# Adaptive modulation moved out of the sparse attention: 192 fp32 matmuls replaced by 192 scaled adds on VectorE and 48 one-column matmuls in the first feed-forward

## The chip, the cores and the metric

One Trainium2 chip, one core of it. The time is the device time of one execution in microseconds (us); the number that counts is the median of the runs.

## The reference, cut to what matters

Two transformer blocks follow each other on a sequence of 1024 tokens of width 1024. The first block has three attention branches and a feed-forward; the second is modulated by a condition vector.

```python
# first block: sliding-window, sparse ("dsa") and memory attention, gated and projected
x = x + einsum("bsd,de->bse", merged, w_out)
h = rmsnorm(x, g_mlp)
x = x + einsum("bsf,fd->bsd", square(relu(h @ w_mlp_in)), w_mlp_out)   # 1024 -> 4096 -> 1024
x = rmsnorm(x, g_final)
# second block
c_act = silu(c)                                   # 1024 numbers
mod = c_act @ w_ada + b_ada                       # (1024) x (1024, 6144) -> 6144 numbers
sh1, sc1, gt1, sh2, sc2, gt2 = split(mod, 6)
x = x + gt1 * mixer(modulate(rmsnorm(x, g_mix), sh1, sc1))
x = x + gt2 * ff(modulate(rmsnorm(x, g_ffn), sh2, sc2))
```

`mod` is a product of one row with a matrix of 24 MB. It depends on nothing that the first block computes, and the second block needs it only when that begins.

## The kernel before

Everything is fp32. The large products run on TensorE (PE) in three passes over split operands: `group` calls `product` (lines 1578 to 1580: high by high, low by high, high by low), 512 columns a pass, and the splits are made by ScalarE (ACT, `split_hi`, line 598: the high part) and VectorE (DVE, `split_lo`, line 972: the rest), from four raw weight tiles of 256 KB that SyncE (SP) loads. A tile is loaded again once its low part is made. The kernel is written by hand: each engine has one program, waits are on semaphores, and the order on each engine and each DMA queue is the order in the code.

**The sparse attention** works in 32 units: eight blocks of 128 queries by four heads. Block b has (b+1) x 128 keys. In turn u the PE program issues `dsa_scores(u+1)` (line 1782), then `dsa_transposes(u-1)` (line 1792), then `dsa_out(u-2)` (line 1804: probabilities by values). DVE masks the scores of unit u (`dsa_masked`: lines 1213 or 1209, the maximum in 1217, its negative in 1218) and normalizes unit u-1 (`dsa_normalized`, lines 1225 and 1226). ACT takes the exponentials of unit u (738) and copies the transposed probabilities of u-1 out of PSUM (748). At the end of a block, ACT copies the output (`oT_hi`, 762) and DVE makes its low part (`oT_lo`, 1237); this DVE step stands between the masking of a unit and the normalization of the one before.

**The modulation before.** In turns 8 to 31, between the scores and the transposes, PE also issues eight fp32 matmuls (line 1817). Each has a 128x24 window of a wide, mostly zero tile with silu(c) in one column as its weights and 256 columns of `w_ada` as its moving operand, so that 24 turns fill a 24x256 tile in `bank3`. The weights come as 24 DMAs of 1 MB on SP's queue (line 346), double buffered against the matmuls; eight loads of attention results (`o_in`, line 349) stand between them, and the first loads of the gates (`stage`, line 363) behind them. After the last unit DVE adds the bias (1245), PE transposes the rows (1826), DVE copies them to `modc` (1247), and only then (`ada_ok`) does PE begin the gated projections; POOL writes the rows to DRAM (`mod_d`, 507), from which two gates are later read back, broadcast to 128 partitions.

**The first feed-forward** (`ff` with k = 0) runs in eight chunks. A chunk has eight groups of 24 passes into `bank0` to `bank3`, one for each hidden tile (two halves of the tokens by four tiles of 128), and 16 groups of 12 passes, two for each of eight token tiles t. ACT takes relu, square and the high part of a hidden tile (791, 793, 797); DVE makes its low part (`hidden`, line 1302), then the low parts of the next chunk's first matrix (972), then adds the 16 results to `xs` (1327). PE may begin a group when DVE has freed the bank (`group_free`, raised in 1329) four groups before. Chunks 1 to 6 are a loop on DVE, chunks 1 to 7 one on PE.

## Time and profile before

| | |
|---|---|
| median of 3 runs | 3069.17 us (3067.54 to 3070.76) |
| the profiled execution | 3071.32 us |
| its span, first to last instruction | 3069.5 us |
| mean granted TensorE clock | 0.957 |
| sparse attention, up to its last `oT_lo` | about 671 to 871.7 us |
| gated projections | 872.9 to about 978 us |
| first feed-forward | about 1100 to 1790 us |

The profile is of one execution. Busy times are shares of its span; PE's ends are modelled, so the distance from start to start is the better measure of a pass. A chain of waits is followed back from the last instruction. The granted clock is a share of 2.4 GHz.

### The profile page before, as it was taken

How to read it: one execution, taken by the hardware profiler on the slowest of the kernel's cores; microseconds unless marked ns; L12 is line 12 of the kernel's file. 1: busy time of each engine (PE TensorE's matmuls, PEld its weight loads, DVE VectorE, ACT ScalarE, POOL GpSimd, SP SyncE). 2: the span in 40 equal slices, each digit the busy share in tenths (PEclk: the TensorE clock that was granted, in tenths of full speed). 3: DMA queues.
4: the chain of work that ended last, by engine and by line, in shares of the span. 5: the costliest groups of instructions: out<-in, count | busy, mean ns of one | idle time of the engine just before them, and what ended most of it. 6: DMA issues, size and time to landing. Idle time of an engine off the chain costs nothing.

```text
span 3069.5 us, 36159 instructions
## 1 busy us (share of the span) xinstructions
PE 2824.8 (92%) x13038; PEld 2257.7 (74%) x13038; DVE 1432.1 (47%) x2841; ACT 927.0 (30%) x1894; POOL 262.3 (9%) x430
## 2 busy tenths in 40 slices
PE   5996799989997989999999989998697999999997
PEld 4764678864575878888888866877686788888886
DVE  5286489973434242333223352335743443443445
ACT  5165232222211242222223343323414222332221
POOL 0222321220023000000000000003100000000000
PEclk9998889989998999999999998999798999999999
DMA  4012122326435110111011112220221111111111
GB/s 158 19 35 67 35 67 94 103 98 228 146 104 187 52 55 28 55 55 55 27 55 55 41 59 72 77 79 29 83 103 35 55 45 38 55 55 38 44 41 62
DMA packets 119646, 213.99 MB, mean 70 GB/s; under 512 B 10852, under 2 KB 39100, under 8 KB 119284
## 3 DMA queue, kind: packets, MB, share of 16 engines
q1 hardware_dynamic: 107188, 185.30, 18.3%
q10 hardware_dynamic: 8064, 14.68, 1.3%
q0 software_dynamic: 4288, 12.64, 1.3%
q8 instruction: 61, 1.00, 0.1%
q14 instruction: 45, 0.37, 0.0%
HBM read 178.94 MB, written 33.64 MB: 69 GB/s over the span
## 4 chain that ended last, share of the span: by engine, by line
PE 78%; DVE 9%; ACT 5%; DMA 3%; issue 2%; POOL 1%; SPq 0%; DVEq 0%; ACTq 0%; POOLq 0%
PE bank L1578 22%; PE bank L1579 22%; PE bank L1580 22%; PE bank L1817 3%; ACT w_hi L598 1%; PE bank L1804 1%; PE bank L1782 1%; DVE w_lo L972 1%; DVE stage L1256 1%; DVE probs L1077 1%; DMA w_raw<-in_w_mlp_in 1%; DMA w_raw<-in_w_ff 1%; PE bank L1792 1%; DVE mx L1063 1%; ACT bank L830 1%
## 5 line engine op out<-in xcount | busy, mean ns | idle before, releaser
L1578 PE MATMUL bank<-h_hi,w_hi 128*128 128x512 f32 (+1 forms) x1312 | 514.0, 392 | 18.3 <-DVE h_lo L1370 7.9
L1579 PE MATMUL bank<-h_lo,w_hi 128*128 128x512 f32 (+1 forms) x1312 | 511.7, 390 | 0.0
L1580 PE MATMUL bank<-h_hi,w_lo 128*128 128x512 f32 (+1 forms) x1312 | 511.2, 390 | 0.0
L598 ACT ACTIVATE w_hi<-w_raw 128x512 fp32r<-128x512 f32 (+3 forms) x440 | 254.9, 616 | 763.4 <-PE bank L1580 551.7
L1578 PE MATMUL bank<-w_hi,hid_hi 128*128 128x512 f32 x1024 | 400.9, 391 | 10.6 <-DVEq L1329 10.2
L1580 PE MATMUL bank<-w_hi,hid_lo 128*128 128x512 f32 x1024 | 399.4, 390 | 0.0
L1579 PE MATMUL bank<-w_lo,hid_hi 128*128 128x512 f32 x1024 | 399.4, 390 | 0.0
L972 DVE TENSOR_TENSOR w_lo<-w_raw,w_hi 128x512 fp32r<-128x512 f32 (+3 forms) x384 | 246.2, 680 | 211.6 <-ACT w_hi L598 205.8
L1302 DVE TENSOR_TENSOR hid_lo<-bank,hid_hi 128x512 fp32r<-128x512 f32 x128 | 88.6, 692 | 512.9 <-ACT hid_hi L797 512.9
L1578 PEld LDWEIGHTS bank<-h_hi,w_hi 128*128 128x128 f32 x1312 | 249.2, 190 | 73.5 <-DVE h_lo L1370 8.7
L1579 PEld LDWEIGHTS bank<-h_lo,w_hi 128*128 128x128 f32 x1312 | 249.2, 190 | 51.0 <-issue 0.7
L1580 PEld LDWEIGHTS bank<-h_hi,w_lo 128*128 128x128 f32 x1312 | 249.1, 190 | 51.0
L1327 DVE TENSOR_TENSOR xs<-xs,bank 128x512 f32<-128x512 f32 x256 | 175.9, 687 | 182.1 <-PE bank L1580 170.9
L1578 PEld LDWEIGHTS bank<-w_hi,hid_hi 128*128 128x128 f32 x1024 | 192.7, 188 | 56.3 <-DVEq L1329 16.9
L1580 PEld LDWEIGHTS bank<-w_hi,hid_lo 128*128 128x128 f32 x1024 | 192.7, 188 | 40.2
L1579 PEld LDWEIGHTS bank<-w_lo,hid_hi 128*128 128x128 f32 x1024 | 192.6, 188 | 39.6
L791 ACT ACTIVATE bank<-bank 128x512 f32<-128x512 f32 x128 | 74.5, 582 | 373.7 <-PE bank L1580 373.7
L1173 DVE TENSOR_SCALAR_CACHE_REDUCE cmpj<-isc,cand 128x384 bf16<-128x384 f32 (+1 forms) x186 | 175.8, 945 | 5.5
L1579 PE MATMUL bank<-hT_lo,w_hi 128*128 128x512 f32 x384 | 149.5, 389 | 0.0
L1580 PE MATMUL bank<-hT_hi,w_lo 128*128 128x512 f32 x384 | 149.5, 389 | 0.0
L1578 PE MATMUL bank<-hT_hi,w_hi 128*128 128x512 f32 x384 | 149.5, 389 | 0.0
L1325 DVE TENSOR_TENSOR bank<-bank,rowv 128x512 f32<-128x512 f32 x128 | 89.5, 699 | 106.6 <-PE bank L1580 94.5
(381 smaller groups left out, 3916.5 us busy)
## 6 DMA issues: line engine op xcount, KB each, us to landing
w_raw<-in_w_ff SPq DMA_DIRECT2D x128, 256.0 KB, 3.1
w_raw<-in_w_in SPq DMA_DIRECT2D x104, 256.0 KB, 2.9
ada<-in_w_ada SPq DMA_DIRECT2D x24, 1024.0 KB, 5.2
w_raw<-in_w_mlp_in SPq DMA_DIRECT2D x64, 256.0 KB, 3.1
w_raw<-in_w_mlp_out SPq DMA_DIRECT2D x64, 256.0 KB, 3.1
gates_scratch<-gstage ACTq DMA_DIRECT2D x48, 256.0 KB, 2.0
stage<-gates_scratch SPq DMA_DIRECT2D x16, 768.0 KB, 5.1
w_raw<-in_w_out SPq DMA_DIRECT2D x32, 256.0 KB, 3.7
```

The costliest lines, as they stand in the source:

```text
L598: A_(W[par][0][:, p, 0:n], raw[:, p % NRAW, 0:n], ACT.Copy).then_inc(w_hi, 1)
L791: A_(x, x, ACT.Relu).then_inc(f_r, 1)
L830: A_(x, x, ACT.Identity, scale=amod[:, a0 + k:a0 + k + 1], bias=modc[:, b0 + k:b0 + k + 1])\
L972: tt(W[par][1][:, p, 0:n], raw[:, p % NRAW, 0:n], W[par][0][:, p, 0:n].bitcast(f32), ALU.subtract).then_inc(w_lo, 1)
L1173: tsc(cmpj[:, 0:(b + 1) * P], isc[b][:, :], cand[:, b - 2:b - 1].bitcast(f32), None, ALU.is_ge, ALU.add, accum_out=cnt[:, b - 2:b - 1]).th ...
L1302: tt(hid[h][1][:, f, :], bank[n % 4][:, :], hid[h][0][:, f, :].bitcast(f32), ALU.subtract)\
L1325: tt(b, b, rowv[:, 512 * m:512 * m + 512], ALU.mult).then_inc(gt_x, 1)
L1327: tt(x, x, bank[(2 * t + m) % 4][:, :], ALU.add).then_inc(x_add, 1)
L1578: mm(out, lh, rh, start=(i == 0), stop=False)
L1579: mm(out, lh, rl, start=False, stop=False)
L1580: last = mm(out, ll, rh, start=False, stop=(i == n - 1))
L1817: l = mm(bank[3][0:NPC, 0:256], cwide[:, k, NPC - 1 - n:2 * NPC - 1 - n], adab[n % 2][:, k, :], start=(n == 0 and k == 0), stop=(n == NPC ...
```

## The change

- The 24 x 8 matmuls, the wide tile, the bias add in rows, the two transposes and the copy at the end of the attention are gone, and so are the 24 DMAs of 1 MB on SP's queue. The eight loads of attention results follow each other there, and the second gate load waits for the selection (`sel_done`) instead of the last of the matmuls.
- POOL now issues 96 DMAs of 256 KB (two row tiles of 128 by 256 columns each) into two small buffers in the place of `rowv`, behind its gate adds and the wait for the end of the attention. From the third on, each waits until DVE has used both row tiles of the load two before.
- In chunks 1 to 6 of the first feed-forward DVE computes four column tiles of 256 in each. A column tile is eight row tiles, each scaled by its number of silu(c) and added into `adac` (128x256). Four row tiles stand behind each of hidden tiles 0 to 5, eight behind tile 6.
- PE sums over the partitions: for each column tile, two matmuls with 128x128 of `adac` as weights and one column of ones, into two columns of `bank4`. They stand behind groups 2, 4 and 6 of the chunk and behind the two groups of token tile 0.
- After the feed-forward DVE adds the bias (now loaded with the other vectors and transposed) to `bank4` in one step. POOL loads the gain `g_final` after the last modulation load, and writes two gates to DRAM from columns, 4 bytes a piece.
- PE's loop is over chunks 1 to 6, and chunk 7 is written out behind it.

```diff
             for b in range(2):
                 sp.wait_ge(at_od[b], 16 * (NSWA + 8))
             sp.wait_ge(group_done, GP)
...
-            for n in range(24):
-                if n >= 2:
-                    sp.wait_ge(ada_mm, n - 1)
-                elif n == 1:
-                    sp.wait_ge(sel_done, 6)
-                sp.dma_start(adab[n % 2][:, :, :], ada[:, :, n * 256:(n + 1) * 256]).then_inc(ada_in[n % 2], 16)
-                if n >= 3 and attended:
-                    h, o, d, k0, k1 = attended.pop(0)
-                    sp.dma_start(o[:, k0:k1, :].bitcast(f32), d[k0 * P:k1 * P, h * HALF:(h + 1) * HALF]
-                                 .rearrange("(k p) q -> p k q", p=P)).then_inc(o_in, 16)
+            for h, o, d, k0, k1 in attended:
+                sp.dma_start(o[:, k0:k1, :].bitcast(f32), d[k0 * P:k1 * P, h * HALF:(h + 1) * HALF]
+                             .rearrange("(k p) q -> p k q", p=P)).then_inc(o_in, 16)
...
                 else:
-                    sp.wait_ge(ada_mm, 24)
+                    sp.wait_ge(sel_done, 6)
...
             pool.wait_ge(d_pv, 32)
+            ada = a["w_ada_2"][0].rearrange("(k p) n -> p k n", p=P)
+            for q in range(96):
+                n, k = q // 4, 2 * (q % 4)
+                if q >= 2:
+                    pool.wait_ge(ada_s, 2 * q - 2)
+                pool.dma_start(adab[q % 2][:, :, :], ada[:, k:k + 2, n * 256:(n + 1) * 256]).then_inc(ada_in[q % 2], 16)
+            pool.wait_ge(ada_s, 192)
             row(rowv, a["g_final"].rearrange("(o n) -> o n", o=1))
+            pool.wait_ge(ada_ok, 1)
...
+                for k in (16, 40):
+                    pool.dma_start(mod_d[k:k + 8, :].rearrange("k p -> p k"), modc[:, k:k + 8]).then_inc(mod_out, 16)
...
+                        if mod and n < 7:
+                            for r in range(4 * n, 4 * n + 4 if n < 6 else 32):
+                                modulation(i, r)
+
+                def modulation(i, r):
+
+                    n, k = r // 8, r % 8
+                    q = r // 2
+                    x = adab[q % 2][:, k % 2, :]
+                    if k % 2 == 0:
+                        dve.wait_ge(ada_in[q % 2], i * 128 + (16 * (q // 2 + 1) - 128))
+                    if k == 0:
+                        dve.wait_ge(ada_mm, i * 4 + (n - 3))
+                        l = tsc(adac[:, :], x, cact[:, 0:1], None, ALU.mult)
+                    else:
+                        l = stt(adac[:, :], x, cact[:, k:k + 1], adac[:, :], ALU.mult, ALU.add)
+                    l.then_inc(ada_s, 1)
+                    dve.wait_ge(ada_s, i * 32 + (r + 1 - 32))
...
+            dve.wait_ge(ada_mm, 25)
+            tt(modc[:, :], bank[4][:, 0:48], cols[:, c_ada:c_ada + 48], ALU.add).then_inc(ada_ok, 1)
+            dve.wait_ge(ada_ok, 1)
...
-                if 8 <= u < 32:
-                    n = u - 8
-                    pe.wait_ge(ada_in[n % 2], 16 * (n // 2 + 1))
-                    for k in range(8):
-                        l = mm(bank[3][0:NPC, 0:256], cwide[:, k, NPC - 1 - n:2 * NPC - 1 - n], adab[n % 2][:, k, :],
-                               start=(n == 0 and k == 0), stop=(n == NPC - 1 and k == 7))
-                    l.then_inc(ada_mm, 1)
...
-                def chunk(i, first):
+                def modulation(i, n):
+
+                    pe.wait_ge(ada_s, i * 32 + (8 * n + 8 - 32))
+                    for e in range(2):
+                        l = mm(bank[4][:, ds(i * 8 + (2 * n + e - 8), 1)], adac[:, e * P:(e + 1) * P], one[:, :],
+                               start=True, stop=True)
+                    l.then_inc(ada_mm, 1)
+
+                def chunk(i, first, last):
+                    mod = not (k or first or last)
...
+                        if mod and n in (2, 4, 6):
+                            modulation(i, (n - 2) // 2)
...
+                            if mod and t == 0 and m == 1:
+                                modulation(i, 3)
```

PE in turns 8 and 9 of the sparse attention. Before:

```order
L1782 MATMUL bank<-k_dT,q_dT 128x384 [waits dsa_s]
L1817 MATMUL bank<-ada_147,silu_c_wide 24x256 [waits ada_in0]
L1817 MATMUL bank<-ada_147,silu_c_wide 24x256 x7
L1792 MATMUL bank<-ident,dsa_probs 128x128 [waits dsa_pt,dsa_p]
L1792 MATMUL bank<-ident,dsa_probs 128x128
L1804 MATMUL bank<-dsa_probsT_141,v_d 64x128 [waits dsa_pt]
L1804 MATMUL bank<-dsa_probsT_141,v_d 64x128
```

And in the changed kernel, where the lines have other numbers:

```order
L1793 MATMUL bank<-k_dT,q_dT 128x384 [waits dsa_s]
L1803 MATMUL bank<-ident,dsa_probs 128x128 [waits dsa_pt,dsa_p]
L1803 MATMUL bank<-ident,dsa_probs 128x128
L1815 MATMUL bank<-dsa_probsT_142,v_d 64x128 [waits dsa_pt]
L1815 MATMUL bank<-dsa_probsT_142,v_d 64x128
```

Nothing stands between the scores of one unit and the transposes of another any more. DVE in a chunk of the first feed-forward, changed kernel, from the last low part of the weights through hidden tile 0 to tile 1 (`ada_148` and `ada_149` are the two load buffers):

```order
L969 TENSOR_TENSOR w_lo<-w_raw,w_hi 128x512 [waits w_hi]
L1290 ISA
L1291 TENSOR_TENSOR hid_lo<-bank,hid_hi 128x512 [waits ff_hi]
L1305 ISA [waits ff_lo]
L1307 ISA [waits ada_in0]
L1308 TENSOR_SCALAR ada_sum<-ada_148,cact 128x256 [waits ada_mm]
L1312 ISA
L1310 SCALAR_TENSOR_TENSOR ada_sum<-ada_148,cact,ada_sum 128x256 [waits ada_sum]
L1312 REGISTER_ALU
L1310 SCALAR_TENSOR_TENSOR ada_sum<-ada_149,cact,ada_sum 128x256 [waits ada_in1,ada_sum]
```

Before, the low part of tile 1 followed that of tile 0 directly; now four row tiles stand between them, each waiting for the one before. PE behind group 2 of such a chunk, changed kernel (`one` is the column of ones):

```order
L1591 MATMUL bank<-h_0_hi,w_lo 128x512
L1861 ISA
L1863 ISA [waits ada_sum]
L1863 MATMUL bank<-one,ada_sum 128x1
L1863 ISA
L1863 MATMUL bank<-one,ada_sum 128x1
L1596 REGISTER_ALU
L1589 MATMUL bank<-h_0_hi,w_hi 128x512 [waits group_free]
```

Two one-column matmuls and a wait on DVE's sums now stand between group 2 and group 3, which followed each other directly.

## Rows read from the trace of the kernel before

**Rows 1.** The page: the chain that ended last, shares of the span by engine

```profile
PE 78%; DVE 9%; ACT 5%; DMA 3%; issue 2%; POOL 1%; SPq 0%; DVEq 0%; ACTq 0%; POOLq 0%
```

**Rows 2.** PE's groups of instructions by line: busy us, mean ns | idle before

```profile
L1817 PE MATMUL bank<-ada,silu_c_wide 128*24 128x256 f32 x384 | 89.2, 386 | 0.0
```

**Rows 3.** Waits, 690 to 870 us: us in total, times, longest

```profile
DVE dsa_probs L1213 <- PE bank L1782: 71.4, 19, 5.5
```

**Rows 4.** Timeline of PE, block of 896 to 1024 keys: start us, us

```profile
829.22 3.63 PE L1817 MATMUL bank<-ada,silu_c_wide 128*24 128x256 f32 x16
832.78 0.98 PE L1792 MATMUL bank<-ident,dsa_probs 128*128 128x128 f32 x7
...
837.28 3.63 PE L1817 MATMUL bank<-ada,silu_c_wide 128*24 128x256 f32 x16
```

**Rows 5.** Timeline of DVE, same turn: masking begins, normalization

```profile
829.33 1.28 DVE L1213 SCALAR_TENSOR_TENSOR dsa_probs<-isc,bank 128x512 f32<-128x512 f32 x2 [4.81 <-PE bank L1782]
...
832.16 0.69 DVE L1226 TENSOR_SCALAR dsa_probs<-dsa_probs,rs 128x896 f32<-128x896 f32 x1
```

**Rows 6.** Timelines of PE and DVE, block of 512 keys

```profile
728.72 0.55 PE L1792 MATMUL bank<-ident,dsa_probs 128*128 128x128 f32 x3
729.20 0.87 PE L1804 MATMUL bank<-dsa_probsT,v_d 128*64 128x128 f32 x6
...
731.05 1.26 PE L1817 MATMUL bank<-ada,silu_c_wide 128*24 128x256 f32 x5
...
725.27 0.69 DVE L1213 SCALAR_TENSOR_TENSOR dsa_probs<-isc,bank 128x512 f32<-128x512 f32 x1 [3.77 <-PE bank L1782]
...
726.97 0.49 DVE L1226 TENSOR_SCALAR dsa_probs<-dsa_probs,rs 128x512 f32<-128x512 f32 x1
```

**Rows 7.** Timeline of the end of the sparse attention

```profile
870.86 0.38 ACT L762 ACTIVATE oT_hi<-bank 128x256 fp32r<-128x256 f32 x1 [2.17 <-PE bank L1804]
871.27 0.42 DVE L1237 TENSOR_TENSOR oT_lo<-bank,oT_hi 128x256 fp32r<-128x256 f32 x1 [9.87 <-ACT oT_hi L762]
...
872.90 0.47 PE L1578 MATMUL bank<-oT_hi,w_hi 128*128 128x512 f32 x1 [0.53 <-DVE modc L1247]
```

**Rows 8.** Windows: us, busy of each engine, PEclk, DMA share, GB/s

```profile
270.00:280.00 10.00, 8.38 (x70) 6.08 (x66) 8.90 (x22) 7.84 (x28) 1.44 (x2) 0.94 0.09 27
...
380.00:400.00 20.00, 15.88 (x44) 12.16 (x42) 11.74 (x22) 9.00 (x22) 0.00 (x0) 0.50 0.00 0
...
700.00:705.00 5.00, 5.00 (x13) 1.77 (x13) 1.75 (x5) 0.00 (x0) 0.00 (x0) 0.53 0.00 0
705.00:710.00 5.00, 5.00 (x24) 2.32 (x23) 1.26 (x3) 0.98 (x3) 0.00 (x0) 1.00 0.55 173
```

**Rows 9.** Timelines of DVE and PE in a chunk of the first feed-forward

```profile
1226.73 0.69 DVE L1302 TENSOR_TENSOR hid_lo<-bank,hid_hi 128x512 fp32r<-128x512 f32 x1 [4.75 <-ACT hid_hi L797]
1227.68 2.50 DVE L972 TENSOR_TENSOR w_lo<-w_raw,w_hi 128x512 fp32r<-128x512 f32 x4 [0.26 <-DVE hid_lo L1302]
...
1235.15 0.68 DVE L1327 TENSOR_TENSOR xs<-xs,bank 128x512 f32<-128x512 f32 x1
...
1235.94 0.50 PE L1578 MATMUL bank<-w_hi,hid_hi 128*128 128x512 f32 x1 [0.23 <-DVEq L1329]
```

**Rows 10.** Timeline of PE: fp32 matmuls with few columns between groups

```profile
1940.72 1.93 PE L1937 MATMUL bank<-mpc,sel8a 8*128 8x17 f32 x16
1942.59 0.50 PE L1578 MATMUL bank<-h_hi,w_hi 128*128 128x512 f32 x1
```

**Rows 11.** Timeline of DVE: a scaled operation on two SBUF tiles; one beside POOL

```profile
639.37 0.62 DVE L1193 SCALAR_TENSOR_TENSOR rel<-rel,cnt,cmpj 128x384 f32<-128x384 f32 x1
...
688.82 1.46 DVE L1226 TENSOR_SCALAR dsa_probs<-dsa_probs,rs 128x256 f32<-128x256 f32 x1
```

**Rows 12.** DMA issues: KB each, median us from issue to landing

```profile
w_raw<-in_w_mlp_in SPq DMA_DIRECT2D x64, 256.0 KB, 3.1
...
rowv<-in_g_final POOLq DMA_DIRECT2D x1, 512.0 KB, 4.7
```

More of the change, by code:

```diff
@@ L98, in build @@
         zero = misc("zero", [P, 1])
+        one = misc("one", [P, 1])
         bg_now = misc("bg_now", [P, 8])
@@ L157, in build @@
         oT = [act_pair("oT0", s0), act_pair("oT1", s1)]
[L158 to L163 removed]
+        ROW0 = mcur[0] - 4096
+        adab = [at(f"ada{i}", [P, 2, 256], f32, ROW0 + 2048 * i) for i in range(2)]
+        adac = at("ada_sum", [P, 256], f32, ROW0 - 1024)
         mT = [act_pair("mT0", s2), act_pair("mT1", s3)]
@@ L520, in mod_row @@
             def mod_row(k):
-                return mod_d.rearrange("(s r) c -> s (r c)", r=4)[k:k + 1, :]
+                return mod_d.rearrange("(s r) c -> s (r c)", r=8)[k:k + 1, :]
             pool.wait_ge(d_pv, 32)
+            ada = a["w_ada_2"][0].rearrange("(k p) n -> p k n", p=P)
[5 more added lines that the diff above has]
+            pool.wait_ge(ada_s, 192)
             row(rowv, a["g_final"].rearrange("(o n) -> o n", o=1))
+            pool.wait_ge(ada_ok, 1)
+            with nc.allow_non_contiguous_dma(reason="two rows of the modulation, from columns"):
+                for k in (16, 40):
+                    pool.dma_start(mod_d[k:k + 8, :].rearrange("k p -> p k"), modc[:, k:k + 8]).then_inc(mod_out, 16)
             pool.wait_ge(n_tr, 56)
@@ L1296, in ff, with hidden @@
             def ff(c0, g0, k, x0, behind, second_half):
-                def hidden(i, n0):
+                def hidden(i, n0, mod=False):
                     for n in range(n0, n0 + 4):
@@ L1823, in _ @@
                     dsa_out(u - 2)
-            pe.wait_ge(ada_r, 1)
-            for j in range(2):
-                l = nc.tensor.transpose(bank[3][:, j * NPC:(j + 1) * NPC], mrows[:, j * P:(j + 1) * P], ident[0:NPC, 0:NPC])
-            l.then_inc(ada_t, 1)
             chunk_ready(C_PD)
@@ L1858, in ff @@
                 pa, pb = c0 % 2, 1 - c0 % 2
-                def chunk(i, first):
+                def modulation(i, n):
[5 more added lines that the diff above has]
+                def chunk(i, first, last):
+                    mod = not (k or first or last)
                     chunk_ready(2 * i + c0)
```

57 lines of the change are left out of this document (21 added, 36 removed).

## The prediction

> **What bounds the kernel now.** I read the chain that ended last first: 78% of the span is PE's [rows 1]. So a matmul that is taken out counts in full, unless something else ends last in its place. PE's lines then show what the modulation costs: 384 passes, 89.2 us busy, and no idle time before them [rows 2]. The waits of that stretch say which engine is short there: DVE's masking waited 71.4 us for PE's scores [rows 3]. PE is the bound of the sparse attention, and DVE and ACT have room.
>
> **Taken out: the 24 packs of matmuls.** In one turn PE starts its 16 passes at 829.22 and the transposes at 832.78 [rows 4], 3.56 us. There are 24 such packs, so 24 x 3.56 = **-85.4**. The first pack ran at a lower clock and took longer (PE was at 0.53 of its clock from 700 to 705 us and at 1.00 from 705 on [rows 8]), but if the clock rises at the same moment, other work stands in those microseconds, so I count this pack at the full rate too.
>
> What becomes late next is a turn's other work. With blocks of 1024 keys PE needs 837.28 - 832.78 = 4.50 us for transposes, values and scores [rows 4]. DVE's masking and normalization run from 829.33 to 832.85, 3.52 us, and with 0.1 us of signalling at each end 3.7 [rows 5]: PE remains the bound. With 512 keys it is 731.05 - 728.72 = 2.33 against 727.46 - 725.27 = 2.19 plus 0.2, so 2.4 [rows 6]: a draw, 0.07 a turn. I allow 0.2 a turn for the three turns of the 384-key block, together 0.9 us.
>
> A second wait comes at block ends. DVE then stands at `oT_lo` until PE has done a set of transposes and values and ACT has copied the result. In the 512-key block these values end about 0.48 + 0.87 = 1.4 us after the scores [rows 6], ACT adds 0.1 + 0.38, DVE 0.1 + 0.35 [rows 7], and normalization another 0.75: 3.1 us instead of 2.4. In the longest block the same sum is about PE's own 4.5. Over six block ends I take 2.7 us. Together **+3.6**; the bounds are 0 (DVE exactly hidden) and 15, which is half a microsecond or so in each turn, if the modelled ends hide latency.
>
> At the end of the attention the bias add, the transposes and the copy go: from `oT_lo`'s end at 871.69 to the first projection at 872.90 [rows 7] is 1.21 us, of which 0.1 remains: **-1.1**. The loads of attention results come earlier and have less company (the DMA engines were busy 0.55 of the time beside the modulation's 24 MB, 705 to 710 us [rows 8]); the second gate load no longer waits. Both lie ahead of need, nothing is gained or lost.
>
> **Put in: PE's one-column matmuls.** No row shows a product of one column. The nearest are 16 fp32 passes of 17 columns between two groups: 1942.59 - 1940.72 = 1.87 us, 0.117 a pass [rows 10]. Two matmuls are four passes, 0.47 us. Since a weight load behind such a short pass isn't hidden and the sequencer takes up a register for the address, I add two more passes' time, about 0.28: **0.75 us an insertion**, with bounds of 0.47 and 1.3 (four passes that each hold PE as long as the step behind a late bank, 0.33). Three insertions of a chunk stand ahead of the last hidden group, where PE never idles: 2.25 us. The fourth stands ahead of the group of token tile 2. There PE already waits for DVE, about 0.38 us, since the low parts of the weights end late: that group started at 1235.94, behind the add that began at 1235.15 [rows 9]. The fourth fills that hole first.
>
> **Put in: DVE's row tiles.** A scaled operation on two SBUF tiles of 384 columns took 0.62 us [rows 11]; 128 columns fewer at about a nanosecond each gives 0.49, and 0.04 for waiting on itself gives 0.53 us a row tile. Four are 2.1 us. Behind a hidden tile DVE was idle 4.75 us [rows 9], so tiles 0 to 5 have room, and PE's wait for eight row tiles is met: it asks one group after the tile's own, 4.75 + 0.69 = 5.44 us later, low part and four row tiles take 2.8 of that, and ACT's three steps on the tile about 0.6 each (0.38 for half the columns [rows 7]), together 4.6.
>
> Tile 6 is the narrow place. Its eight row tiles need four loads, and only two can be there. Row tiles 24 and 25 end 1.0 us after the low part, the third load is issued then, and lands about 3.1 us later (256 KB on SP's queue took that; 512 KB on POOL's took 4.7 [rows 12]). The fourth follows 1 us behind. So the last row tile ends about 6.1 us after the low part of tile 6, where that of tile 7 would begin 4.75 us later, or with the insertion ahead of it 5.5 us later: 0.7 late. DVE had 0.26 us in hand before the weights' low parts [rows 9], and these, the reloads behind them and the first add all move with it: 0.45 us late. The hole ahead of token tile 2 is then 0.38 + 0.45 = 0.83 us, the insertion of 0.75 lies inside it, and the chunk pays 0.45. A chunk: 2.25 + 0.45 = 2.7 us; six of them, **+16.2**. Bounds: three insertions of 0.47 and no lateness give 8; insertions of 1.3 and both loads in 4.7 us make the last row tile 2.1 us late and a chunk 3.9 + 2.1 = 6.0, six of them 36. I stay near the lower end, since the load size has its own row and the pass time its own.
>
> Weighing a rule: the third load's descriptors are made while DVE works on row tiles 26 and 27. A DVE step beside POOL's arithmetic did stretch: 1.46 us for 256 columns [rows 11], where 896 took 0.69 [rows 5]. The Trainium skill (SBUF — State Buffer, section "SBUF: two separate sides") says that a DVE step in a two-port mode locks GpSimd out, so that a DMA issued from there waits for its descriptors. By it the third load would be late by two row tiles, 1.1 us, and the sum would be 6.6 us higher. Only the first row tile of eight is a step on one tensor, so I keep my number and leave the rest to the range.
>
> **Around it.** After the feed-forward DVE has one small step and its own wait more ahead of the norm, **+0.3**. POOL's queue waits until chunk 6 is done; behind it `g_final` is needed only in chunk 7's token tile 4, more than a whole set of eight hidden groups later (8 x 5.44 us), and the other steps later still. The gates written in 4-byte pieces are read only after the second block's mixer. Covered; if they were not, DVE would stand at `row_in`.
>
> **The sum.** -85.4 + 3.6 - 1.1 + 16.2 + 0.3 = **-66.4 us**. The profiled execution took 3071.3 us, so 3004.9; it stood 2.1 above the median, so the median should be 3069.2 - 66.4 = **3003 us**. A measurement of this kernel tells some 0.2% (6 us) from no change.
>
> **The rivals.**
>
> *The insertions or tile 6 cost two to three times as much.* The loads land late by turns and every chunk's adds start late, or PE drains at each wait on `ada_sum`, since its sequencer is let go only shortly before the array runs dry. For it: DVE's chain into token tile 2 has no slack today [rows 9]. Against: 4.75 us of idle time behind each hidden tile. At 6 us a chunk: 3003 + 6 x 3.3 = 3023. Chance 0.17.
>
> *The sparse attention becomes bound by the chain through three engines.* For it: the draw at 512 keys. Against: DVE's 71 us of waiting were PE's alone. At 0.7 us a turn in 24 turns instead of 3.6 in all: 3003 + 13 = 3016. Chance 0.13.
>
> *The clock stays low in the sparse attention (the slower side).* Place: 700 us on, where PE is at 0.53 and the packs, its densest work, are gone. From 700 to 870.8 us [rows 7] PE's other work is 170.8 less the packs, 85.4 and some 2 more for the first at the low clock: 83 us. At half the clock it would take that much more, the 3.6 of waits would vanish, and the kernel would come to 3003 + 79 = 3082, slower than before. It decides from about 66 us of such loss, four fifths of the stretch. For it: in the index scores PE was busy 15.88 of 20 us and the clock was at 0.50 [rows 8]. Against: there PE waited for DVE each time; in the memory attention, at 270 to 280 us, with short transposes and products like these, the clock was at 0.94 [rows 8]. The Trainium skill (TensorE: Matmul & The Clock Gate, Part 4) says that transposes don't count as work for the gate. Transposes are a fifth of a turn here (0.98 of 4.5 us [rows 4]), and the 0.94 arose in a stretch that has them too. Chance 0.03 for all of it; and 0.05 for a rise that comes late by 20 to 40 us, 3013 to 3023.
>
> *The change does nothing there* is excluded: the built order has no matmul between scores and transposes.
>
> **How the numbers follow.** The forecast has 0.62. The range 2992 to 3030 takes in the lower bounds (8 for the chunks and 0 for the attention: 3003 - 8.2 - 3.6 = 2991) and the first two rivals and most of the late clock; it leaves out the low clock and the far ends, about 0.1. Faster by over 0.2% is all but these: 0.95; within 0.2% 0.02; slower 0.03.
>
> **What would show it.** PE's time without modulation in a 1024-key turn stays 4.5 us; the attention, from 700 us to its last low part, takes about 88 us instead of 171; the granted clock is at 1.00 from about 705. A row tile takes about 0.5 us, an insertion 0.75 from start to start; chunks 1 to 6 each last 2.7 us longer than before, chunk 7 as before. Wrong would be: PE waiting on DVE's masking in every turn, a clock of 0.5 beyond 715 us, or chunks longer by 5 us.

## The result, and the profile after

The changed kernel takes **3037.33 us** (median of 4 runs, 3034.59 to 3040.61), the kernel before 3068.91 us (median of 4, 3067.54 to 3070.76): ratio **0.990, 95% interval 0.9885 to 0.9909**. It is 31.6 us faster. I had predicted 3003 us, 66 us faster, with a range from 2992 to 3030: the direction was right, but only half of the gain came, and the time lies outside the range.

The profiled execution of the changed kernel took 3035.8 us, with a span of 3033.7 us (3069.5 before). Four landmarks split the two spans: the first pass of the gated projections, the first low part of a hidden tile of the first feed-forward, the first transpose of the norm behind it, and the end.

| stage | before, us | after, us | difference | predicted |
|---|---|---|---|---|
| up to the gated projections | 872.9 | 797.3 | **-75.6** | -82.9 |
| projections, up to the first hidden tile | 219.9 | 220.9 | +1.0 | 0 |
| first feed-forward | 707.5 | 751.2 | **+43.6** | +16.2 |
| the rest | 1269.1 | 1264.3 | -4.8 | +0.3 |

The rest lasted between 1261.8 and 1270.2 us in the eleven runs below, all with the same code there, so the -4.8 is the spread of executions. Of the -75.6, 1.4 us is such spread too: the attention's first scores start at 669.83 us before and at 668.43 after. From there to the first projection it is 203.07 and 128.83 us, 74.2 less. Two stages are to be explained: nearly 9 us of the attention's gain that did not come, and 27 us that the feed-forward took too much.

**The sparse attention.** Windows of the changed kernel (us, busy us of each engine, granted clock of PE as a share, DMA share, GB/s):

```profile
700.00:710.00 10.00, 10.00 (x26) 4.80 (x25) 4.93 (x15) 3.60 (x10) 0.00 (x0) 0.50 0.19 70
710.00:720.00 10.00, 10.00 (x28) 5.22 (x28) 5.23 (x12) 2.73 (x7) 0.00 (x0) 0.50 0.00 0
720.00:725.00 5.00, 5.00 (x16) 2.83 (x16) 2.95 (x9) 2.16 (x6) 0.00 (x0) 0.50 0.00 0
725.00:730.00 5.00, 5.00 (x24) 3.33 (x24) 2.47 (x8) 1.50 (x4) 0.00 (x0) 0.80 0.00 0
730.00:740.00 10.00, 9.68 (x55) 6.54 (x54) 8.23 (x20) 5.98 (x14) 0.00 (x0) 1.00 0.11 26
```

Before, PE had 0.53 of its clock from 700 to 705 us and all of it from 705 on [rows 8]. Now it has half (1.2 instead of 2.4 GHz) until about 727 us. The transposes of turns 8 and 15 bound the stretch, first before, then after:

```profile
706.12 0.44 PE L1792 MATMUL bank<-ident,dsa_probs 128*128 128x128 f32 x2
747.06 0.65 PE L1792 MATMUL bank<-ident,dsa_probs 128*128 128x128 f32 x4
```

```profile
699.12 0.69 PE L1803 MATMUL bank<-ident,dsa_probs 128*128 128x128 f32 x2
727.83 0.66 PE L1803 MATMUL bank<-ident,dsa_probs 128*128 128x128 f32 x4
```

Before, the same work and seven packs took 40.94 us, 15.96 without the packs (24.98). Now it takes 28.71: the clock costs 12.75 us. Against that, the first pack, at the low clock, had taken 5.59 us and not the 3.56 counted, and all 24 were 87.6 us, so 2.2 more went away than predicted. The turn itself is as predicted. PE, block of 1024 keys:

```profile
780.51 1.09 PE L1803 MATMUL bank<-ident,dsa_probs 128*128 128x128 f32 x8
781.53 1.74 PE L1815 MATMUL bank<-dsa_probsT,v_d 128*64 128x128 f32 x14
783.20 1.98 PE L1793 MATMUL bank<-k_dT,q_dT 64*128 64x512 f32 x4
785.11 1.09 PE L1803 MATMUL bank<-ident,dsa_probs 128*128 128x128 f32 x8
```

785.11 - 780.51 = 4.60 us, for the 4.50 of [rows 4]. The waits of PE between 640 and 800 us are few:

```profile
PE bank L1803 <- DVE dsa_probs L1223: 13.8, 7, 7.4
PE bank L1589 <- DVE oT_lo L1234: 1.1, 1, 1.1
```

The kernel before has 12.6 us of the first kind in its own attention, so 1.2 us of new waits. Turn by turn, from one start of the transposes to the next and without the packs, the other turns at the full clock are equal to within 0.1 us, except at three block ends (0.1 to 0.4 us longer) and in the last turn but one (0.8 longer): 1.6 us in all, where I had 3.6. So the attention's balance against my 82.9 is 12.8 of clock, 2.2 more taken out, 2.0 less of waits and 0.15 more at its end: 8.7 us.

**The first feed-forward.** Here are the waits of PE inside chunks 1 to 6, first before, then after (`DVEq` is DVE's sequencer, which frees the banks):

```profile
PE bank L1578 <- DVEq L1329: 1.2, 4, 0.4
```

```profile
PE bank L1589 <- DVEq L1337: 12.4, 6, 2.5
PE bank L1863 <- DVE ada_sum L1310: 10.6, 6, 1.9
```

Each of the six chunks has two new stalls. The second of the two rows is one that I had called covered. DVE at the start of chunk 2 shows why it is there:

```profile
1214.10 0.69 DVE L1291 TENSOR_TENSOR hid_lo<-bank,hid_hi 128x512 fp32r<-128x512 f32 x1 [1.12 <-ACT hid_hi L794]
1215.26 0.35 DVE L1308 TENSOR_SCALAR ada_sum<-ada,cact 128x256 f32<-128x256 f32 x1 [0.47 <-DVE hid_lo L1291]
1215.64 1.52 DVE L1310 SCALAR_TENSOR_TENSOR ada_sum<-ada,cact,ada_sum 128x256 f32<-128x256 f32 x3
1217.29 0.69 DVE L1291 TENSOR_TENSOR hid_lo<-bank,hid_hi 128x512 fp32r<-128x512 f32 x1
1219.56 1.00 DVE L1310 SCALAR_TENSOR_TENSOR ada_sum<-ada,cact,ada_sum 128x256 f32<-128x256 f32 x2 [1.57 <-DMA ada<-in_w_ada]
1220.89 1.00 DVE L1310 SCALAR_TENSOR_TENSOR ada_sum<-ada,cact,ada_sum 128x256 f32<-128x256 f32 x2 [0.33 <-DMA ada<-in_w_ada]
```

Hidden tiles 0 and 1 do not come 5.44 us apart here, but 3.2 (1214.10 and 1217.29): ACT and DVE have just split the second matrix of the chunk and are late for tile 0. The trace of the kernel before has the same two at 1191.22 and 1194.09, before the even distance of 5.44 begins. Row tiles 0 to 3 use up the two loads in stock, the next two are issued only then, and DVE waits for them until 1219.56 and 1220.89. PE asks for the sum right behind group 2:

```profile
1219.99 0.39 PE L1591 MATMUL bank<-h_hi,w_lo 128*128 128x512 f32 x1
1222.06 0.60 PE L1863 MATMUL bank<-one,ada_sum 128*128 128x1 f32 x4 [1.68 <-DVE ada_sum L1310]
1222.52 0.48 PE L1589 MATMUL bank<-h_hi,w_hi 128*128 128x512 f32 x1
```

From start to start this wait is 2.07 - 0.23 = 1.84 us, and 1.71 to 2.06 in the other chunks: 11.5 us in six. An insertion that is not late costs little:

```profile
1233.27 0.40 PE L1591 MATMUL bank<-h_hi,w_lo 128*128 128x512 f32 x1
1233.50 0.50 PE L1863 MATMUL bank<-one,ada_sum 128*128 128x1 f32 x4
1233.87 0.47 PE L1589 MATMUL bank<-h_hi,w_hi 128*128 128x512 f32 x1
1234.18 0.39 PE L1590 MATMUL bank<-h_lo,w_hi 128*128 128x512 f32 x1
```

Without it the last of these would start at 1233.27 + 2 x 0.227 = 1233.72; it is 0.46 us later, for the 0.75 that I had taken.

At the end of the chunk the eight row tiles behind hidden tile 6 are late by more than I had worked out. DVE:

```profile
1246.94 0.69 DVE L1291 TENSOR_TENSOR hid_lo<-bank,hid_hi 128x512 fp32r<-128x512 f32 x1 [2.48 <-ACT hid_hi L794]
1247.93 0.35 DVE L1308 TENSOR_SCALAR ada_sum<-ada,cact 128x256 f32<-128x256 f32 x1 [0.30 <-DVE hid_lo L1291]
1248.32 1.52 DVE L1310 SCALAR_TENSOR_TENSOR ada_sum<-ada,cact,ada_sum 128x256 f32<-128x256 f32 x3
1252.28 1.00 DVE L1310 SCALAR_TENSOR_TENSOR ada_sum<-ada,cact,ada_sum 128x256 f32<-128x256 f32 x2 [2.43 <-DMA ada<-in_w_ada]
1253.66 1.00 DVE L1310 SCALAR_TENSOR_TENSOR ada_sum<-ada,cact,ada_sum 128x256 f32<-128x256 f32 x2 [0.38 <-DMA ada<-in_w_ada]
1254.79 0.69 DVE L1291 TENSOR_TENSOR hid_lo<-bank,hid_hi 128x512 fp32r<-128x512 f32 x1
```

The last row tile ends 7.0 us after the low part of tile 6 (at 1254.66; I had 6.1), and the low part of tile 7 starts 1.9 us after ACT's high part was there (ACT's step of 0.60 us began at 1252.24). The low parts of the weights, their reloads and the adds all follow late, and PE stands ahead of token tile 2. In the next chunk:

```profile
1355.18 0.39 PE L1591 MATMUL bank<-w_hi,hid_lo 128*128 128x512 f32 x1
1357.64 0.50 PE L1589 MATMUL bank<-w_hi,hid_hi 128*128 128x512 f32 x1 [2.07 <-DVEq L1337]
...
1358.87 0.63 PE L1590 MATMUL bank<-w_lo,hid_hi 128*128 128x512 f32 x1
1359.29 0.63 PE L1591 MATMUL bank<-w_hi,hid_lo 128*128 128x512 f32 x1
1359.72 0.63 PE L1589 MATMUL bank<-w_hi,hid_hi 128*128 128x512 f32 x1
```

Two things are to be seen. The stall is 2.46 - 0.23 = 2.23 us. And behind it the passes start 0.43 us apart instead of 0.23. The windows say what that is:

```profile
1358.00:1360.00 2.00, 2.00 (x7) 1.61 (x6) 1.39 (x3) 0.00 (x0) 0.00 (x0) 0.60 0.72 243
1360.00:1362.00 2.00, 2.00 (x6) 1.52 (x6) 0.49 (x1) 0.00 (x0) 0.00 (x0) 0.54 0.00 0
1362.00:1364.00 2.00, 2.00 (x11) 1.65 (x10) 0.69 (x1) 0.00 (x0) 0.00 (x0) 1.00 0.00 0
```

PE's clock fell to half for some 3.5 us after the stall, and came back. The stalls ahead of token tile 2 in chunks 1 to 6 are 2.51, 1.87, 2.23, 2.63, 2.32 and 1.74 us; the clock fell behind the first, third, fourth and fifth, for 7 or 8 passes each, 30 passes x 0.2 = 6 us in all. The stalls at the first column tile were followed by no fall.

The sum of the chunks: insertions 24 x 0.46 = 11.0, the first column tile 11.5, token tile 2 13.3 less the 2.5 that it already had before, and the slow passes 6: 39.3 of the 43.6 us. Of the rest, 2.4 us stand in the run without any modulation work too (none, below).

### The profile page after: what moved, and what is told of

Its sections match the earlier page's. It is cut to its first block, busy times and chain, and to the rows that moved or that the text cites. A ratio compares the mean times of both kernels' runs of the same rounds, so it can differ in the third digit from the quotient of the medians.

```text
span 3033.7 us, 36160 instructions
## 1 busy us (share of the span) xinstructions
PE 2768.6 (91%) x12748; PEld 2239.5 (74%) x12748; DVE 1521.9 (50%) x3032; ACT 929.3 (31%) x1894; POOL 332.8 (11%) x526
## 4 chain that ended last, share of the span: by engine, by line
PE 72%; DVE 12%; DMA 6%; ACT 5%; issue 3%; POOL 1%; SPq 0%; DVEq 0%; ACTq 0%; POOLq 0%
PE bank L1589 21%; PE bank L1591 21%; PE bank L1590 21%; DVE w_lo L969 2%; DMA ada<-in_w_ada 2%; PE bank L1793 1%; PE bank L1815 1%; DVE ada_sum L1310 1%; ACT w_hi L595 1%; DVE stage L1247 1%; DMA w_raw<-in_w_mlp_in 1%; DVE probs L1074 1%; DMA w_raw<-in_w_ff 1%; PE bank L1803 1%; DMA w_raw<-in_w_mlp_out 1%
```

## Experiments

All kernels ran beside the kernel before, on the same chip in one session for each of the three groups. Its medians there were 3069.1, 3070.0 and 3070.0 us. "Feed-forward" is the third stage of the table above, read from each run's profile; it tells a few microseconds better than the whole time, since the moment at which the clock rises in the attention differs from run to run. In the seven runs whose attention has the changed kernel's code, it rose 58 to 59 us after the first scores in five, and the attention lasted 128.7 to 128.9 us up to the first projection; in pe_only and one_load it rose 69 us after them, and the attention lasted 133.9 and 133.7.

| run | median, us | ratio to before (95%) | to projections | feed-forward |
|---|---|---|---|---|
| before | | | 872.9 | 707.5 |
| the change | 3037.3 | 0.990 (0.9885 to 0.9909) | 797.3 | 751.2 |
| none | 2999.9 | 0.977 (0.9756 to 0.9789) | 802.3 | 709.9 |
| pe_only | 3008.2 | 0.980 (0.9786 to 0.9819) | 801.3 | 721.5 |
| rows_only | 3026.2 | 0.986 (0.9847 to 0.9880) | 796.3 | 734.7 |
| one_load | 3011.4 | 0.981 (0.9798 to 0.9831) | 801.2 | 720.7 |
| shift | 3007.7 | 0.979 (0.9780 to 0.9807) | 799.8 | 718.7 |
| four | 3014.7 | 0.982 (0.9806 to 0.9834) | 799.5 | 725.7 |
| fill | 3042.5 | 0.991 (0.9895 to 0.9924) | 801.3 | 752.0 |
| shift_fill | 3004.2 | 0.979 (0.9779 to 0.9808) | 796.3 | 719.3 |
| kick | 2999.1 | 0.977 (0.9752 to 0.9779) | 791.6 | 719.4 |
| fill_8 | 3001.5 | 0.978 (0.9765 to 0.9792) | 793.8 | 719.6 |
| fill_turns | **2993.8** | **0.975** (0.9739 to 0.9766) | 788.6 | 717.8 |

My theory after reading the trace (A): the feed-forward loses by loads that land late, at two places, and by the clock that falls behind the stalls; the one-column matmuls cost only themselves. The rivals: PE drains at each insertion (B, the rival of the prediction), and DVE's own time for the row tiles costs (C).

**none.** The row tiles, the loads and the insertions are left out of the feed-forward, and `modc` is the bias alone:

```diff
-                        if mod and n < 7:
-                            for r in range(4 * n, 4 * n + 4 if n < 6 else 32):
-                                modulation(i, r)
...
-                        if mod and n in (2, 4, 6):
-                            modulation(i, (n - 2) // 2)
```

> The modulation is left out of the first feed-forward altogether (no loads, no row tiles, no one-column matmuls; the second block is modulated by the bias alone), so this shows what the removal in the sparse attention brings by itself. All theories: the first projection starts at about 797 us as in the changed kernel, 75.6 us earlier than before, so some 2993 to 2995 us, and the first feed-forward's chunks last 87.6 us as before. If it comes out at 2986 or less, the attention's loss of clock was tied to the new code, if at 3010 or more, something outside the feed-forward costs time too.

2999.9 us: 69 us below the kernel before, and 5 us above what I expected. The profiled execution was the slowest of the four (3005.0). It came to the attention 5.1 us later than the changed kernel did (first scores at 673.56), which is why the projections begin at 802.3 and not at 797.3; the attention itself lasted 128.7 us, as in the changed kernel. What the other three lost is not known. The feed-forward is at 709.9, as before (707.5). So the modulation's work costs 751.2 - 709.9 = 41.3 us there. That is what the next three runs take apart.

**pe_only.** The insertions alone, without their wait; the loads and row tiles are left out as in none, and the sum tile is filled with zeros:

```diff
-                    pe.wait_ge(ada_s, i * 32 + (8 * n + 8 - 32))
```

> The 48 one-column matmuls stay at their places, but wait for nothing, and the loads and row tiles are left out (the sum tile holds zeros). Theory A (an insertion costs only its own 0.46 us, the rest of the feed-forward's loss comes from loads that land late): 24 x 0.46 = 11 us above the kernel without any modulation work, about 3004 to 3006. Theory B (the array drains at each insertion, whoever is late): an insertion costs 1 us and more, 3018 or above. Theory C (VectorE's own time for the row tiles is what costs): as A.

The feed-forward takes 11.6 us more than in none, for 24 x 0.46 = 11.0. B falls: 48 matmuls at their places cost half a microsecond for two.

**rows_only.** Loads and row tiles alone, nobody asks for the sums:

```diff
-                        dve.wait_ge(ada_mm, i * 4 + (n - 3))
...
-                        if mod and n in (2, 4, 6):
-                            modulation(i, (n - 2) // 2)
```

> Loads and row tiles stay, the one-column matmuls are left out, and nobody waits for the sums. Theory A: the waits at the first column tile (11.5 us in six chunks) and the insertions (11) go, but the eight row tiles behind hidden tile 6 still end 2 to 2.5 us after the moment at which the low part of hidden tile 7 could start, so token tile 2 waits 2 us or more in each of six chunks, and where it does the clock falls for some 3 us: 13 to 22 us above the kernel without modulation work, 3007 to 3016. Theory B: no more than 3 us above it, under 2998. Theory C: as A.

The feed-forward takes 24.8 us more than in none, above the 13 to 22 expected; the mechanism is the one expected, and stronger. Waits of PE in the feed-forward:

```profile
PE bank L1587 <- DVEq L1336: 18.0, 6, 3.4
```

Six stalls of 2.8 to 3.6 us from start to start (2.2 on the mean in the changed kernel): without insertions hidden tile 7 is there half a microsecond sooner after tile 6, and the row tiles are not. The clock fell behind five of them (not behind the 2.96 us of chunk 2); 36 passes started about 0.43 apart, which is another 7 us. So one late place, without any insertion, costs 25 us.

**one_load.** Everything is at its place, but each buffer is loaded once and the same numbers are read again:

```diff
-            for q in range(96):
-                n, k = q // 4, 2 * (q % 4)
-                if q >= 2:
-                    pool.wait_ge(ada_s, 2 * q - 2)
-                pool.dma_start(adab[q % 2][:, :, :], ada[:, k:k + 2, n * 256:(n + 1) * 256]).then_inc(ada_in[q % 2], 16)
+            for q in range(2):
+                pool.dma_start(adab[q % 2][:, :, :], ada[:, 2 * q:2 * q + 2, 0:256]).then_inc(ada_in[q % 2], 16)
...
-                    if k % 2 == 0:
-                        dve.wait_ge(ada_in[q % 2], i * 128 + (16 * (q // 2 + 1) - 128))
+                    if k < 4 and k % 2 == 0:
+                        dve.wait_ge(ada_in[q % 2], 16)
```

> Row tiles and one-column matmuls with their waits for each other stay, but each of the two buffers is loaded once, and the row tiles read the same data again (so the sums are not the reference's). This takes the landing of the loads away and keeps VectorE's time. Theory A: only the insertions are left, 11 to 13 us above the kernel without modulation work, 3004 to 3007, no wait of the one-column matmuls above 0.5 us. Theory B: 3018 or above, since the insertions and waits are all there. Theory C: the row tiles take VectorE as long as before, so as slow as the changed kernel, 3025 or above.

The feed-forward takes 10.8 us more than in none: the insertions, and nothing else. PE has no wait in chunks 1 to 6 any more. DVE does the same 192 row tiles, with the same waits of DVE and PE for each other. C falls. The 30 us that the changed kernel has above this run are all tied to the loads: to the moment at which they land, or to their traffic, which is gone here too. The next run tells the two apart.

**shift.** Same work, same two buffers, other places. No row tile stands behind hidden tile 0, four behind each of tiles 1 to 6, and eight in the output phase, where DVE is idle 2.03 us between two adds:

```diff
-                        if mod and n < 7:
-                            for r in range(4 * n, 4 * n + 4 if n < 6 else 32):
+                        if mod and 1 <= n < 7:
+                            for r in range(4 * n - 4, 4 * n):
...
+                        if mod and 2 <= t < 6:
+                            for r in (20 + 2 * t, 21 + 2 * t):
+                                modulation(i, r)
...
-                        if mod and n in (2, 4, 6):
-                            modulation(i, (n - 2) // 2)
+                        if mod and n in (3, 5, 7):
+                            modulation(i, (n - 3) // 2)
...
-                            if mod and t == 0 and m == 1:
+                            if mod and t == 7 and m == 0:
                                 modulation(i, 3)
```

> Same work, same two buffers, other places: no row tile behind hidden tile 0, four behind each of hidden tiles 1 to 6, two behind each of token tiles 2 to 5; the one-column matmuls behind groups 3, 5 and 7 and inside token tile 7. Theory A (the loss is loads that land late, because the sums are asked for right behind hidden tiles 0 and 1, whose low parts come late and close together, and because tile 6 has eight row tiles): waits at the first column tile and ahead of token tile 2 vanish, and with them the falls of the clock; the insertions alone stay: as the kernel with the matmuls alone, 3006 to 3011. Rival D (VectorE's row tiles delay PE wherever they stand, by the loads' company on the DMA queues or by the low parts of the weights): 3020 or more.

3007.7 us, and the feed-forward at 718.7: 32.5 us less than in the change, and no more than the insertions cost alone. The window over the feed-forward, first of this run, then of the changed kernel:

```profile
1112.00:1700.00 588.00, 587.79 (x2636) 486.92 (x2634) 267.85 (x457) 162.26 (x279) 68.48 (x95) 1.00 0.30 91
```

```profile
1112.00:1700.00 588.00, 565.04 (x2495) 464.47 (x2494) 256.41 (x441) 149.36 (x256) 68.49 (x95) 0.99 0.29 89
```

PE is busy 587.8 of 588 us, with its full clock. Rival D (the row tiles or loads delay PE wherever they stand) falls with it, and with it the traffic of the loads, since all 96 are there.

**four.** The order of the change, but four buffers of one row tile in the same 4 KB:

```diff
-                if q >= 2:
-                    pool.wait_ge(ada_s, 2 * q - 2)
-                pool.dma_start(adab[q % 2][:, :, :], ada[:, k:k + 2, n * 256:(n + 1) * 256]).then_inc(ada_in[q % 2], 16)
+                if q >= 4:
+                    pool.wait_ge(ada_s, q - 3)
+                pool.dma_start(adab[q % 4][:, :], ada[:, k, n * 256:(n + 1) * 256]).then_inc(ada_in[q % 4], 16)
```

> The order of the changed kernel with four buffers of one row tile (192 loads of 128 KB) in the same 4 KB, so that a load is issued behind each row tile instead of each second. Theory A: the sum of the first column tile is ready about 1 us earlier (the wait of 1.9 falls to about 0.9), the last row tile behind hidden tile 6 about 1.2 us earlier (the stall at token tile 2 falls from 2.2 to about 1), and the clock does not fall any more: 37 less 6 x 2.2 and 7 us, so 3016 to 3022. Rival D: no gain, 3034 or above. If a load's time is its start-up and not its bytes, 128 KB lands no sooner than 256 KB, which is assumed here.

3014.7 us, slightly better than expected; the feed-forward is at 725.7. The wait at the first column tile is at most 0.56 us (expected 0.9), the stall at token tile 2 at most 0.78 (expected 1). The reason is in the list of DMA issues, first of this run, then of the changed kernel:

```profile
ada<-in_w_ada POOLq DMA_DIRECT2D x192, 128.0 KB, 2.4
```

```profile
ada<-in_w_ada POOLq DMA_DIRECT2D x96, 256.0 KB, 3.2
```

I had assumed that half the bytes land no sooner. They do, by 0.8 us, and the next load is issued behind one row tile instead of two. That there are twice as many DMAs shows in no wait here: POOL has no other work.

**fill.** The changed kernel with nine fp32 matmuls that nobody reads, inside PE's two long waits for DVE's selection (3.3 and 7.4 us):

```diff
+            def filler(m):
+                for _ in range(m):
+                    mm(bank[3][:, 0:512], ident[:, :], k_dT[:, 0:512], start=True, stop=True)
...
+                if u in (1, 2):
+                    filler(3 if u == 1 else 6)
```

> The changed kernel with nine fp32 matmuls (128x128 by 512 columns, into bank3, which nobody reads) on TensorE inside its two long waits at the start of the sparse attention (3.3 and 7.4 us, for VectorE's selection). Theory A (the attention ran at half clock from 680 to about 727 us because PE had stood idle there, and rose later than before because the packs were gone): the clock stays at or near 1.00 through these stretches, PE's 512- and 384-key turns fall from 4.3 and 3.4 us towards VectorE's 2.4 and 2.2, and the attention ends 8 to 15 us sooner: 3022 to 3030. Rival E (short matmuls and transposes let the clock fall again by themselves): the clock is at 0.50 again by 700 us and the time within 3 us of 3037, or up to 7 us above it if the nine matmuls run at the low clock.

3042.5 us: a miss, nothing gained. The windows show how far it went:

```profile
680.00:685.00 5.00, 2.53 (x8) 0.90 (x6) 4.79 (x9) 0.59 (x3) 5.00 (x3) 1.00 0.33 105
685.00:690.00 5.00, 5.00 (x14) 2.23 (x12) 3.85 (x16) 3.06 (x10) 1.25 (x2) 0.57 0.79 229
```

The clock held through the waits (without the nine it was at 0.50 from 675 us on, as the shift run shows) and fell right behind the 2.47 us in which PE still stood idle. It stayed at 0.50 until after 730 us. So rival E is right in effect for this run: holding the clock up to 685 us is worth nothing if it then falls.

**shift_fill.** Both edits together.

> Both edits together: the row tiles at the new places and the nine matmuls in PE's waits. They touch different stretches, so the gains should add: theory A 2993 to 3000; with rival E 3006 to 3015.

3004.2 us, below shift by 3.5 us, which the intervals do not separate (0.9780 to 0.9807 against 0.9779 to 0.9808). In the profiled execution the clock rose at 722 us, 52 us after the first scores instead of 59, and the attention lasted 125.9 us instead of 128.8. A small gain of the filler, up to those 3 us, is neither shown nor excluded.

**kick.** The order of shift, nothing in the long waits, but four such matmuls in turn 8, where the first pack of the modulation stood before:

```diff
+                if u == 8:
+                    filler(4)
```

> The version with the row tiles at their new places, and four fp32 matmuls (128x128 by 512 columns, unread) on TensorE in turn 8 of the sparse attention, where the first pack of the modulation stood in the kernel before; nothing in the long waits. Theory A (the clock rose at 705 us before because the packs were long, uninterrupted matmuls, and rises 18 to 25 us later without them): the clock is at 1.00 from about 706 to 712 us instead of 725 to 730. The four take 4 x 1.8 = 7.2 us at half clock and give some 8 us back, so the time stays within 3 us of 3007.7. Rival E (the rise has its own moment, whatever stands in turn 8): the clock rises at 725 us or later and the time goes up by 7 us, to 3013 to 3016.

2999.1 us, 8.6 less than shift, with intervals that just part (0.9752 to 0.9779 against 0.9780 to 0.9807); I had expected a draw. The windows:

```profile
695.00:700.00 5.00, 5.00 (x11) 2.19 (x12) 1.97 (x6) 1.09 (x3) 0.00 (x0) 0.50 1.05 388
700.00:705.00 5.00, 5.00 (x9) 1.93 (x9) 1.47 (x5) 0.00 (x0) 0.00 (x0) 0.67 0.51 190
705.00:710.00 5.00, 4.38 (x23) 2.38 (x22) 2.91 (x8) 2.61 (x8) 0.00 (x0) 1.00 0.00 0
```

The clock rises while the four run (they took 5.4 us instead of 7.2), to 1.00 by 705 us, as in the kernel before and some 25 us sooner than in shift (0.55 from 725 to 730 us). It rose 34 us after the first scores, where none of the seven runs with the attention's own work alone has it before 58. Long matmuls at that place are enough to bring the rise forward, and the kernel before had them there: this is the missing gain of the attention. From the first scores to the first projection it is 122.6 us, 6.2 less than in shift, with the four already paid; the other 2 us by which the projections begin sooner lie ahead of the attention. Work that nobody needs made the kernel some 0.2 to 0.3% faster.

**fill_8.** Both edits, with eight matmuls instead of six in the second long wait.

> As the version with both edits, but eight matmuls instead of six in PE's second long wait, since with six PE still stood idle for 2.47 us there and the clock fell right behind it. Theory A: a pause of 2 us or more is what the fall follows; with 0.7 us left the clock stays at 1.00 beyond 685 us, and the attention ends 8 to 13 us sooner, so 2991 to 3000. Rival E: the waits for the masking in the next turns (0.6 and 1.3 us, with PE busy 1.1 of 2.2 us a turn at the full clock) bring it down before 700 us all the same: 3001 to 3006.

3001.5 us, at the edge between the two expectations, and E describes it. The clock fell all the same, at 685.6 us (0.56 between 685 and 690 us), ahead of the largest wait that is left in the attention (1.3 us, up to 689.46). The waits between the eight matmuls and the fall are 0.75, 0.37 and 0.2 us, with PE busy for 3.88 us between 680 and 685 us, in short pieces. That contradicts what I had written of the pause that a fall follows. The attention lasted 125.7 us, 3 less than without filler, as in shift_fill.

**fill_turns.** As fill_8, and one matmul more in each of turns 3 to 11:

```diff
+                if 3 <= u < 12:
+                    filler(1)
```

> As the previous one, and one such matmul more in each of turns 3 to 11. Theory A: PE has no pause above 1 us before the 512-key blocks, the clock stays at 1.00 through them, a turn of 384 or 512 keys takes 2.4 to 2.7 us instead of 3.2 and 4.3, and the attention ends 5 to 12 us sooner than with both edits alone: 2992 to 2999. Rival E (it falls anyway): nine matmuls at half clock cost 9 x 1.8 = 16 us: 3015 to 3022.

**2993.8 us**, the best of all: 2.5% below the kernel before (0.9739 to 0.9766) and 43 us below the change. Windows:

```profile
685.00:690.00 5.00, 4.95 (x18) 2.20 (x18) 3.86 (x17) 1.94 (x10) 1.12 (x1) 1.00 0.68 203
700.00:705.00 5.00, 5.00 (x21) 2.52 (x20) 2.93 (x10) 2.44 (x7) 0.00 (x0) 1.00 1.04 384
```

The clock never falls in the attention. A turn of 512 keys takes 2.3 to 2.5 us (scores at 709.94, 712.26 and 714.72) instead of 4.3 at half clock. PE waits for DVE 0.8 us in all from 700 to 732 us, so the draw of the prediction (2.33 against 2.4 us a turn [rows 6]) stands.

## Why the prediction was right and wrong

**Right: what the removal is worth per turn.** The -85.4 rested on 24 packs of 3.56 us, and the turn of 1024 keys without a pack is 4.60 us. The new waits came to 1.6 us (predicted 3.6), and at the attention's end the -1.1 came to -0.95: `oT_lo` ends at 797.00 and the projection starts at 797.26. (The 0.35 us that the prediction gives DVE's `oT_lo` is 0.42 in [rows 7]; it moves the waits by less than half a microsecond.) SP's and POOL's queues and the gates cost nothing that shows: the second stage lasts 219.9 before and 220.1 to 221.1 in all runs.

**Wrong: "if the clock rises at the same moment".** This step of the first term failed. I had a rise late by 20 to 40 us as a side rival with 0.05; it came 22 us late and cost 12.8 us, 10.6 after the 2.2 by which the packs were worth more, at the lower end of the 10 to 20 given there. The kick run shows the cause: long matmuls in turn 8 bring the rise back to 705 us, and the attention ends 6.2 us sooner. My argument against it took two stretches with other patterns [rows 8] and did not ask what PE had been doing in the microseconds just ahead of 705 us, where the answer stood: the first pack. The Trainium skill (TensorE: Matmul & The Clock Gate, Part 4) says that transposes don't count as work for the gate. The trace neither confirms nor contradicts it: in the turn of 1024 keys shown above 1.0 of 4.6 us are transposes, at a clock of 1.00, and in a turn of 512 keys 0.83 of 4.31 us (710.12 to 710.95), at 0.50. The share is the same, a fifth, so it does not set the two stretches apart. What did hold the clock down from 700 to 727 us stays open.

**Wrong: the 2.7 us of a chunk.** It was 43.6 / 6 = 7.3, and the parts below make up 6.5 of it:

- *Three insertions of 0.75.* They cost 0.46 each, four passes of 0.117 as in [rows 10]. The two more passes that I added for weight loads and the sequencer do not exist. And the fourth did not vanish in the hole ahead of token tile 2, since that was full of the lateness: 4 x 0.46 = 1.8 instead of 2.25.
- *"Tiles 0 to 5 have room, and PE's wait for eight row tiles is met."* This was wrong for tiles 0 and 1, at 1.9 us a chunk, the largest single error. I took the distance of 5.44 from the middle of a chunk. At its start the low parts stand 2.9 us apart in the trace of before too, and I had counted DVE's time, not the loads: row tiles 4 to 7 wait for two loads that cannot be issued before row tiles 1 and 3. The one_load run shows that DVE's time was indeed covered.
- *Tile 6, 0.7 late, 0.45 paid.* It was 1.9 late. The last row tile came 7.0 us after the low part instead of 6.1, since I had left out the steps around a load (0.30 us from the low part to the first row tile, 0.29 from the end of a row tile to POOL's issue), and hidden tile 7 was there 5.2 us after it, not 5.5. The stall at token tile 2 grew by 1.8 us a chunk. A subtraction of two large numbers (6.1 - 5.5) was given as 0.7 with no error of its own, where each side was good to half a microsecond.
- *Not in the sum at all:* the clock falls behind a stall of PE. In four of six chunks this cost 1.5 us, 6 us in all, and 7 in rows_only.

**The rivals.** "The insertions or tile 6 cost two to three times as much" is what came, 7.3 us a chunk where it had 6, but by its first half (loads that land late by turns) and not by its second: pe_only and one_load rule out that PE drains at each insertion. That attention and feed-forward could both go wrong at once was not in the range: 3023 for the one and 3013 to 3023 for the other add up to about the 3037 that came. The attention bound by three engines did not come, and the clock that stays low all through did not either. Two of the signs that I had named for being wrong were there: a clock of 0.5 beyond 715 us, and chunks longer by more than 5 us.

**The rule that was weighed.** The Trainium skill (SBUF — State Buffer, section "SBUF: two separate sides") would have POOL's descriptors wait for a DVE step in a two-port mode. I had put its price at 1.1 us for the third load of tile 6 and left it out. The trace shows no such wait: POOL issued that load at 1249.10, 0.3 us behind the row tile, took 0.72 us for it as for all 96, and it landed 3.1 us after the issue, with DVE on row tiles 26 and 27 meanwhile. Those two are steps on two tensors; whether one on a single tensor would have delayed it, this load does not tell.

## What to carry to other kernels

A double buffer of small loads covers DVE's time, not the latency of a load: where more steps stand in a row than there are loads in stock, count issue, landing and signalling for each, and put the steps where the distance to the one who asks is long, not where the engine is idle most. Read the distances at the place itself, since the start and the end of a loop body run by other distances than its middle. And before a dense piece of TensorE's work is taken out, look at whether the granted clock rose during it: here it did, and without it 16.0 us of work took 28.7 at half the clock. Four matmuls that nobody reads gave 6 to 9 us of that back.

## What the runs showed of the hardware

- PE's granted clock fell to half within 1.3 us after stalls of 2.2 to 2.6 us between dense passes, and was back about 3.5 us later; after the other stalls of the same loop, of 1.7 to 2.1 us, it did not fall, and in rows_only it did not after one of 2.96 us either. In the attention it fell behind waits of at most 0.75 us (fill_8). In the changed kernel it stayed at half from 695 to 725 us, with PE busy for 30.00 of the 30 us. The same code had it back 58 to 59 us after the first scores in five runs and 69 us after them in two.
- A load of 256 KB from POOL's queue landed 3.2 us after its issue (median of 96), one of 128 KB 2.4 (median of 192), and POOL spent 0.72 and 0.54 us on issuing one. The Trainium skill (DMA: Bandwidth & Descriptors, section "Anatomy of one DMA — SWDGE (gpsimd) path") gives 2.0 us and the bytes at 436 GB/s, by which I estimate 2.6 and 2.3; the smaller one agrees, the larger took 0.6 us more, which no run here explains.
- Two fp32 matmuls of one column, with 128x128 weights each, cost a dense stream of passes 0.46 us, weight loads, a wait that is met and a register address included.
